# Merge gates of a two-layer hybrid backbone, projected in pairs by seven block products instead of eight

## What is computed

```
z  = h @ W_in                              # one projection, columns split among branches and gates
a  = rwkv_output(...) @ w_out              # branch 0
b  = silu(layer_norm(conv(u))) @ conv_out  # branch 1
c  = (u * spatial(v)) @ sgu_out            # branch 2
g  = sigmoid(z[..., OFF_GATE:].reshape(B, T, 3, D_MODEL))
m  = a * g[:, :, 0] + b * g[:, :, 1] + c * g[:, :, 2]
x += gate1 * (m @ w_merge)                 # then a SwiGLU feed-forward with a residual
```

## Time and profile before

| what | value |
|---|---|
| median of three runs | 4149.8 us |
| the profiled execution | 4152.08 us, its span 4150.3 us |
| mean granted TensorE clock | 0.985 |
| PE, PEld busy | 3975.9 us (96%), 2534.4 us (61%) |
| DVE, ACT, POOL busy | 1542.6, 1125.3, 306.6 us |
| HBM read, written | 273.36 MB, 13.63 MB |

### The profile page before, as it was taken

The page is one execution under the profiler, slowest core; times in us unless marked ns, Lnnn a source line. Parts: engine busy times, 40 slices in busy tenths (PEclk is TensorE's granted clock), DMA queues, the critical chain, the costliest instruction groups (busy, mean ns, idle before and its releaser), DMA issues.

```text
span 4150.3 us, 110547 instructions
## 1 busy us (share of the span) xinstructions
PE 3975.9 (96%) x51248; PEld 2534.4 (61%) x51248; DVE 1542.6 (37%) x2525; ACT 1125.3 (27%) x1957; POOL 306.6 (7%) x244
## 2 busy tenths in 40 slices
PE   7999999999999999999999989999998999999999
PEld 3566666666555555655545756666666434478887
DVE  3555665555930001322210255555555310022211
ACT  3444444443021000200000244444444221020100
POOL 0000000000020000122200000000000010004310
PEclk8999999999999999999999989999999999999999
DMA  5000000001432212211123400000010252232244
GB/s 201 25 9 24 24 24 24 29 23 31 151 131 98 92 59 63 80 61 61 52 81 101 151 25 9 23 23 23 23 33 29 101 190 96 87 113 90 90 131 155
DMA packets 80937, 294.10 MB, mean 71 GB/s; under 512 B 9184, under 2 KB 13536, under 8 KB 80096
## 3 DMA queue, kind: packets, MB, share of 16 engines
q1 hardware_dynamic: 72576, 252.74, 18.9%
q10 hardware_dynamic: 6624, 29.04, 1.8%
q0 software_dynamic: 1280, 5.24, 0.3%
HBM read 273.36 MB, written 13.63 MB: 69 GB/s over the span
## 4 chain that ended last, share of the span: by engine, by line
PE 91%; ACT 4%; issue 2%; DVE 2%; DMA 1%; ACTq 0%; DVEq 0%; SPq 0%
PE psum L659 21%; PE psum L1024 16%; PE psum L1436 15%; PE psum L1392 12%; PE psum L908 12%; PE psum L920 5%; PE psum L1056 2%; PE psum L650 2%; PE psum L868 2%; PE psum L792 1%; DMA ring<-w_stream_in 1%; PE psum L886 1%; ACT arena L1799 1%; ACT arena L1805 0%; ACT arena L1812 0%
## 5 line engine op out<-in xcount | busy, mean ns | idle before, releaser
L1024 PEld LDWEIGHTS psum<-arena 32*32 32x32 f32 (+3 forms) x40512 | 698.5, 118 | 359.7 <-issue 283.6
L659 PE MATMUL psum<-arena,ring 128*128 128x512 f32 (+1 forms) x2416 | 878.1, 523 | 10.5 <-DVE arena L2262 3.8
L1024 PE MATMUL psum<-arena 32*32 32x32 f32 (+4 forms) x40512 | 789.5, 208 | 87.7 <-issue 53.3
L659 PEld LDWEIGHTS psum<-arena,ring 128*128 128x128 f32 x2416 | 456.3, 190 | 443.4 <-issue 400.1
L908 PE MATMUL psum<-arena,ring 128*128 128x512 f32 (+1 forms) x1408 | 577.0, 527 | 3.4 <-ACT arena L1624 1.6
L1392 PE MATMUL psum<-arena,ring 128*128 128x256 f32 (+1 forms) x1920 | 518.1, 432 | 0.0
L1392 PEld LDWEIGHTS psum<-arena,ring 128*128 128x128 f32 x1920 | 364.8, 190 | 153.4 <-issue 116.2
L1436 PE MATMUL psum<-arena 128*128 128x384 f32 (+1 forms) x1344 | 368.6, 433 | 0.0
L908 PEld LDWEIGHTS psum<-arena,ring 128*128 128x128 f32 x1408 | 241.1, 192 | 143.8 <-issue 117.0
L1436 PEld LDWEIGHTS psum<-arena 128*128 128x128 f32 x1344 | 255.4, 190 | 106.4
L1436 PE MATMUL psum<-arena,ring 128*128 128x384 f32 (+1 forms) x1008 | 278.5, 433 | 0.0
(11 more groups left out here) (139 smaller groups left out, 3241.2 us busy)
## 6 DMA issues: line engine op xcount, KB each, us to landing
ring<-w_stream_in SPq DMA_DIRECT2D x472, 512.0 KB, 3.7
x_spill<-arena ACTq DMA_DIRECT2D x2, 3072.0 KB, 8.7
arena<-x_spill ACTq DMA_DIRECT2D x16, 384.0 KB, 4.7
arena<-ya_spill ACTq DMA_DIRECT2D x6, 768.0 KB, 6.2
ring<-w_stream_in ACTq DMA_DIRECT2D x8, 512.0 KB, 6.4
arena<-x_in ACTq DMA_DIRECT2D x1, 3072.0 KB, 14.3
arena<-ups_in SPq DMA_DIRECT2D x16, 192.0 KB, 2.4
ya_spill<-arena POOLq DMA_DIRECT2D x8, 384.0 KB, 6.9
```

The source lines that it names most:

```text
L659: mm = eng.matmul(psum[0:lhs[k].shape[-1], tile, a - off:b - off], lhsT=lhs[k], rhs=rhs[k][:, a:b], start=(k == 0), stop=(k == len(lhs) - ...
L1024: return pe.matmul(out, lhsT=lhs, rhs=rhs, start=start, stop=stop, skip_group_check=True)
```

## The change

The 24 gate tiles of a layer become 12 pairs `G{b}{i}` (tiles 2i and 2i+1 of branch b) with seven products each, in the order 1, 6, 5, 7, 2, 3, 4, into the four banks of PSUM tiles 0 and 1. Both chunks of a pair must have arrived; the first is free after product 2, the second after product 4. VectorE forms four sums of h once per layer and six combinations per pair; ScalarE copies product 1 and takes three sigmoids per pair (two halves and one whole tile). GpSimd forms four sums of weights per pair, in one set of buffers (the feed-forward has two), so `w1`, `w3` and `w4` of a pair wait for products 5, 7 and 3 of the pair before. The parts get fixed PSUM tiles. The order of work is redrawn around the pairs. All eight reloads of x are issued after the last pair, since the sums of h lie where x goes.

```diff
+GSUM, GWSUM, GMIX = 36, 8, 61
+GATE_A, GATE_B = (56, 58, 20), (57, 35, 21)
...
-    entry("g00")
+    entry("G00")
     entry("svar", 6)
...
-    for name in ("p00", "g10", "g20"):
-        entry(name, 2)
-    entry("p20")
+    entry("p00", 2)
+    entry("G10", 4)
+    entry("p01")
     out.append(f"t{mod_thirds(l)[1]}")
-    for name in ("cmean", "g01", "cvar"):
+    for name in ("cmean", "G20", "cvar", "G01", "p20", "p21", "p10", "p11"):
         entry(name)
-    merge = ["p01", "p10", "g11", "g21", "p11", "p21"]
-    for q in range(2, KT):
-        merge += [f"g0{q}", f"p0{q}", f"g1{q}", f"g2{q}", f"p1{q}", f"p2{q}"]
-    for n, name in enumerate(merge):
-        entry(name, 1)
...
+    for i in range(1, KT // 2):
+        a, b = 2 * i, 2 * i + 1
+        if i > 1:
+            entry(f"G0{i}", 2)
+        else:
+            out.extend(itertools.islice(mods, 2))
+        entry(f"p0{a}", 1)
+        entry(f"G1{i}", 2)
+        entry(f"p0{b}", 1)
+        entry(f"G2{i}", 2)
+        for name in (f"p2{a}", f"p2{b}", f"p1{a}", f"p1{b}"):
+            entry(name)
...
+GATE_PRODUCTS = (1, 6, 5, 7, 2, 3, 4)
...
+            at.update(p00=2, p01=2, p20=0, p21=2, p10=2, p11=0, cmean=3, cvar=3)
+            for i in range(1, KT // 2):
+                for n, (name, q) in enumerate((("p0", 0), ("p0", 1), ("p2", 0), ("p2", 1), ("p1", 0), ("p1", 1))):
+                    at[f"{name}{2 * i + q}"] = (2, 2, 2, 0, 2, 1)[n]
...
+                for pair in pairs_of_gates(l):
+                    first, second = rows_of(pair)
+                    done[first], done[second] = B["PE"].at(f"{pair}.2"), B["PE"].at(f"{pair}.4")
+                for q in range(KT):
+                    done[f"p2{q}"] = B["PE"].at(f"p1{q}")
...
+                def gate_pair(name):
+                    first, second = (chunk[n] for n in rows_of(name))
+                    take(0, A.at(f"{name}l"))
+                    take(1, V.at(f"{name}d21"))
+                    arrived(pe, key, first)
+                    arrived(pe, key, second)
+                    for i in GATE_PRODUCTS:
...
+                        if i in (5, 6, 7):
+                            pe.wait_ge(*V.at("h4"))
+                            pe.wait_ge(*G.at(f"{name}w{i - 4 if i > 5 else 1}"))
+                        if i == 2:
+                            pe.wait_ge(*A.at(f"{name}c"))
+                            pe.wait_ge(*G.at(f"{name}w4"))
+                        if i == 3:
+                            pe.wait_ge(*V.at(f"{name}b4"))
+                        if i == 4:
+                            pe.wait_ge(*V.at(f"{name}b3"))
...
                 rsqrt(slot(NT, c0), psum[:, 3, 0:n], 1.0 / CONV, eps_c(1), "cln", "cr", A)
+                gate_copy("G01")
                 tables(SILU)
...
-                tables(SIGMOID)
+                gate_sigmoids("G01")
...
+                act.wait_ge(*PE.at(f"G2{KT // 2 - 1}.4"))
+                for j in range(KT):
+                    reload_x(j)
...
+                    k = added.index(name) if b else 0
+                    if k >= 2:
+                        dve.wait_ge(*G.at(added[k - 2].replace("p", "m")))
...
+                def gate_weights(name):
+                    first, second = (chunk[x] for x in rows_of(name))
+                    arrived(pool, f"branch{l}", first)
+                    arrived(pool, f"branch{l}", second)
...
                 summed("sa", lambda j: A.at(f"sv{j}"), H1 + 1, [SV + j for j in range(CT)])
+                gate_weights("G00")
                 summed("sq", lambda j: A.at(f"ssq{j}"), H1, [H1 + j for j in range(CT)])
+                gate_weights("G10")
                 summed("ya", lambda j: V.at(f"y{j}_{len(conv_taps(l)) - 1}"), NT, [CY + j for j in range(CT)])
+                gate_weights("G20")
+                gate_weights("G01")
                 summed("yq", lambda j: A.at(f"csq{j}"), CU[0], CU)
...
+                upcoming = iter(pairs[4:])
+                for name in flow[flow.index("G01"):]:
+                    if name[0] == "G":
+                        following = next(upcoming, None)
+                        if following:
+                            gate_weights(following)
+                    elif name in added:
+                        merge_add(name)
```

More of the change, by code:

```diff
@@ L288, in merge_flow, with rows_of @@
     return flow[flow.index("p00"):]
-def merge_steps(l):
-    return ["g00"] + [n for n in merge_flow(l) if n[0] in "gpc"]
+def rows_of(pair):
+    b, i = int(pair[1]), int(pair[2])
+    return f"g{b}{2 * i}", f"g{b}{2 * i + 1}"
 def flow_chunks(l):
@@ L299, in flow_chunks @@
     for n in whole_flow(l):
-        if n[0] in "mg" or n[:2] in ("cb", "ca", "su", "sv", "p0") and n != "svar":
+        if n[0] == "G":
+            out.extend(rows_of(n))
+        elif n[0] == "m" or n[:2] in ("cb", "ca", "su", "sv", "p0") and n != "svar":
             out.append(n)
@@ L759, in _ @@
                 done = {name: early.at(l, 2 * n + 1) for n, name in enumerate(EARLY)}
-                loads(f"branch{l}", B["chunks"], lambda name: done[name] if name in done else B["PE"].at("p10" if name == "p20" else name))
+                for pair in pairs_of_gates(l):
[3 more added lines that the diff above has]
+                    done[f"p2{q}"] = B["PE"].at(f"p1{q}")
+                loads(f"branch{l}", B["chunks"], lambda name: done[name] if name in done else B["PE"].at(name))
                 for key, names in (("res1", res1_chunks), ("ffn", phases["ffn"]["chunks"]), ("res2", res2_chunks)):
@@ L1898, in branch_phase @@
                     act.activation(slot(VTK[j], 0, n), psum[:, tiles[f"tr{j}"], 0:n], ACT.Copy).then_inc(*A.mark(f"tr{j}"))
-                tables(SIGMOID)
-                act.wait_ge(*V.at(f"u{CT - 1}"))
-                for name in ("g00", "g10", "g20"):
-                    gate(name)
+                gate_sigmoids("G00")
+                gate_copy("G10")
+                gate_sigmoids("G10")
                 copied(mod_thirds(l)[1])
@@ L2427, in branch_phase @@
+                h_sums()
                 for j in range(1, CT):
@@ L2451, in branch_phase @@
                 part("p00")
-                part("p20")
+                gate_sums("G10")
+                part("p01")
                 mod_ready(mod_thirds(l)[1])
                 centred("cmean", 3, CY)
+                gate_sums("G20")
+                gate_sums("G01", second=False)
                 scaled("cn", "cr", CY, NT)
+                gate_sums("G01", first=False)
                 flow = merge_flow(l)
-                for name in flow[flow.index("cvar"):]:
+                for name in flow[flow.index("G01") + 1:]:
                     if name[0] == "p":
                         part(name)
+                    elif name[0] == "G":
+                        gate_sums(name)
                     elif name == "t3":
@@ L2576, in branch_phase, with merge_add @@
                 before = {}
-                for name in parts_of_merge():
-                    b, q = int(name[1]), int(name[2])
-                    if not b:
-                        continue
+                def merge_add(name):
+                    k, q = added.index(name), int(name[2])
                     m, mine = slot(M0[q], c0), name.replace("p", "m")
```

195 lines of the change are left out of this document (152 added, 43 removed).

## The result

Over 13 runs each, on one chip, the changed kernel has a median of 4166.56 us (4153.69 to 4174.07) and the kernel before 4150.74 us (4144.03 to 4161.59). The ratio is 1.0033, 95% interval 1.0022 to 1.0045: about 14 us slower. The forecast was 0.8 us less than before, 4149, with no change as the likeliest outcome. The measured time lies inside the stated range, but it moved the other way, and into the part (slower than 4162) that had 0.27.

A forecast was written before the change was run, and what follows sets the result against it. TensorE's instruction time plus idle bounds the kernel (busy 96%); 51 us of columns and 16 of other savings go into 59 of waits and 7 of clock, total -0.8: 4149 us, range 4127 to 4172.

The forecast's parts named there:

- The pairs: Gate tiles: seven products take 18.07 us (layer 0) and 12.08 (layer 1); twelve pairs save 31.1 and 20.0 us.
- G00: First pair: second chunk lands 1.3 us later, product 6 waits for weight sum w2; 2.2 and 2.5 us.
- G10: Branch 1's first pair: second chunk can be issued only when p00 ends, plus w2; 3.1 and 4.0 us.
- m2.15 and p01: Behind G10: modulation chunk m2.15 (m5.15) and p01's chunk wait for loads issued late; 3.8 us each layer.
- cvar: After G20: GpSimd forms yq only behind G01's weight sums, so cvar waits 5.1 and 4.3 us.
- p20, p10, G02, G03: p20 awaits G01's first sigmoid; the others await a VectorE read freeing their PSUM tile; sum 3.5 and 3.8 us.
- p02: Largest wait: G11's load, GpSimd's four weight sums, m20, then VectorE's p10 precede p02; 14.5 and 8.1 us.
- the chain through m20: Faster rival: p02's wait on GpSimd's m20 is absent or covered; 4124 us; chance 0.22.
- wait that hangs on a load: Slower rival: bunched loads before G00, G10, p01, G11 land 3.0 us late each, +24, 4173 us; chance 0.22.
- res1 did not wait for x: After the last pair: eight reloads of x costed at nothing; res1 waiting for x would show the forecast wrong.
- The clock: Half-rate work behind m2.15/p01, cvar and p02 in each layer: 1.44 us each, 8.6 in all, 7.2 net.
- the old wait: Layer 0 before the change: late chunk's 3.87 us of idle, with 1.44 of clock loss behind it, both to go.

The follow-up runs named there:

- `best`: Changed kernel with GpSimd adding m20 and followers before G11's sums, yq before G01's sums, and modulation chunks spread behind tr1, tr3, sp3: 0.9886 of before, 4105.88 us.
- experiment 2: Changed kernel with TensorE's waits at six places filled by matmuls of constants, results overwritten: 0.9994 of before, 16 to 18 us under the changed kernel.

## Why the prediction was wrong

**The pairs were right.** 18.06 us in layer 0 and 12.09 in layer 1, against 18.07 and 12.08 expected. One pair waits inside, G10 of layer 1, for 0.90 us on POOL (counted in the table below); no later pair waits for POOL or the ring.

**The waits were right, each within 1.1 us, and in sum.** Expected 32.2 and 26.5 us of added waits; the trace has 30.5 and 24.4:

| wait | expected, layer 0 / 1 | measured |
|---|---|---|
| G00 | 2.2 / 2.5 | 1.80 / 1.95 |
| G10 | 3.1 / 4.0 | 2.63 / 3.54 |
| m2.15 and p01 | 3.8 / 3.8 | 3.99 / 3.74 |
| cvar | 5.1 / 4.3 | 4.91 / 4.14 |
| p20, p10, G02, G03 | 3.5 / 3.8 | 2.45 / 3.44 |
| p02 | 14.5 / 8.1 | 14.76 / 7.54 |

Neither strong rival came: the chain through m20 is there, and no wait that hangs on a load was longer than forecast by more than 0.3 us. res1 did not wait for x.

**The step that failed is "The clock".** It charged 1.44 us for each of three stretches per layer, +7.2 in all after the old wait's 1.44, priced from one wait of 3.87 us, and left out G00 and G10. The work behind the waits, held against the same work undisturbed, lost this much (both rows of a pair's start counted, and cvar with the product behind it):

| lost to the clock, us | layer 0 | layer 1 |
|---|---|---|
| G00 | 0.2 | 3.0 |
| G10 | 1.8 | 0.2 |
| p01 | 2.5 | 2.9 |
| cvar | 1.8 | 1.8 |
| p02 | 2.9 | 1.7 |

(Undisturbed, the rows of a pair's start take 2.74 and 7.90 us in layer 0 and 1.89 and 5.34 in layer 1, a part 10.59 and 7.13, cvar 1.45 and 1.02.) That is about 19 us where the forecast had 8.6 for the new stretches. Two measurements that do not use these rows agree: PE is busy for 18.6 us longer than in `best`, and experiment 2 gave back 16 to 18. A dip cost 1.7 to 3.0 us, not 1.44. The length of a wait does not tell whether one comes: G00 of layer 1 lost 3.0 after 1.95 of idle and G10 of layer 0 lost 1.8 after 2.63, while G10 of layer 1 lost 0.2 after 2.64 and a further 0.90. The Trainium skill's rule that the forecast quoted (TensorE: Matmul & The Clock Gate, "Why this matters for your kernels"), and set aside with "some 6 us longer", came nearer (14.6), though of the four entries that it would have added only two paid. The forecast's range allowed the clock 0 to 6 us beyond its term; the term was 10 too small.

In the branch phases the account closes. PE's idle time grew by 45.3 us where the forecast had 58.7 - 8.6 = 50.1, and its busy time fell by 38.8 where it had 58.1 less 7.2 of clock, 50.9. The waits, 4.8 better, hid part of the clock's miss: -0.8 - 4.8 + 12.1 = +6.5, and measured is +6.6. Of the 12.1, 10 are the clock, and about 2 are other terms, each a little off. That the total still fell inside the range owes something to this cancelling.

**A step that was missing.** The forecast put stages whose code stays at nothing, without a reason. They were 6.9 us longer in the profiles, and account for the other half of the 14. In layer 0 the change shortens TensorE's stream by 144 instructions, which moves layer 1's recurrent stage from offset 87 to 31, and its unexplained idle time rose by 11.7 us, of which 4.1 show as a longer stretch. Whether the offset is the cause of those microseconds stays open, as does the cause of the 2.9 ahead of smean of layer 0, which lie within the scatter of single profiles (the rest runs from 2871.8 to 2892.2 in one and the same kernel).

## What to carry to other kernels

An eighth fewer matmul columns was a real saving of 51 us, and it was given away in 55 us of waits of an in-order engine and 19 us of slow work behind them; reordering two lists and spreading the loads brought most of it back (0.9886). Cost a wait of TensorE at its length plus what the half-speed work behind it may lose (1.7 to 3.0 us at eight places here, behind waits of 2 to 15 us, and 0.2 at two others), and look first for the one entry on a helper engine's list that stands behind a load. When a small difference can't be found where the change is, look at the idle rows without a releaser in the stages that only follow it, but hold them against busy time and the ratio before calling them the cause.

## What was not expected of the hardware

TensorE's idle time without a releaser stands at a fixed step of 256 of its instructions (about 127.5 matmul records with their weight loads) in all 18 profiles. In a stage of short matmuls it costs up to 3.6 us a time and came to anything from 29 to 49 us in all, with the offset of the stream. And TensorE worked at a granted clock of 0.71 for the 10 us behind the wait of 14.76 us, and at 1.00 where matmuls on constants filled that wait.
